# Two decoder layers on one core: the attention heads' projections and value rows as three rounded products instead of one f32 product, and where the splitting is done

## The reference, cut to what matters

```
a = h @ w_qkv_a
c_q  = rmsnorm(a[..., :384]);  c_kv = rmsnorm(a[..., 384:640]);  k_pe = rope(a[..., 640:])
q = (c_q @ w_q_b)              # per head: 128 plain columns, 64 rotary ones (then rope)
q_lat = q[..., :128] @ w_uk    # w_uk, w_uv: the two halves of a head's w_kv_b (256 x 256)
...
s = q_lat @ c_kv.T + q_pe @ k_pe.T;  p = softmax(causal(s * scale));  o = (p @ c_kv) @ w_uv
x = x + o @ w_o
```

## Time and profile before

| | us |
|---|---|
| median of 3 runs | 3307.57 |
| lowest, highest | 3305.08, 3314.09 |
| profiled execution, its own time | 3305.95 |
| span of the profiled execution | 3304.1 |
| TensorE busy | 3176.3 |
| VectorE, ScalarE, GpSimd busy | 1840.6, 1333.0, 1204.4 |

### The profile page before, as it was taken

The page is one execution under the profiler, slowest core; times in us unless marked ns, Lnnn a source line. Parts: engine busy times, 40 slices in busy tenths (PEclk is TensorE's granted clock), DMA queues, the critical chain, the costliest instruction groups (busy, mean ns, idle before and its releaser), DMA issues.

```text
span 3304.1 us, 69890 instructions
## 1 busy us (share of the span) xinstructions
PE 3176.3 (96%) x25744; PEld 2883.2 (87%) x25744; DVE 1840.6 (56%) x3139; ACT 1333.0 (40%) x2785; POOL 1204.4 (36%) x841
## 2 busy tenths in 40 slices
PE   8999999999999999999999999999999999999998
PEld 6688887687999999997999887877788899999998
DVE  3466663216544478757303377777734644457885
ACT  2244445512444533322213365566521354443332
POOL 0000000010766777731222222223213276677771
PEclk9999999999999999999999999999989999999999
DMA  3122224500444544432213201110152155454442
GB/s 112 43 79 66 69 74 147 179 13 20 151 157 157 184 133 142 133 109 69 90 53 114 99 14 34 33 40 27 31 170 51 46 164 157 157 184 141 140 141 77
DMA packets 306260, 330.39 MB, mean 100 GB/s; under 512 B 54350, under 2 KB 287745, under 8 KB 305954
## 3 DMA queue, kind: packets, MB, share of 16 engines
q1 hardware_dynamic: 300178, 308.64, 29.4%
q0 software_dynamic: 5904, 19.21, 1.8%
HBM read 232.05 MB, written 116.16 MB: 105 GB/s over the span
## 4 chain that ended last, share of the span: by engine, by line
PE 71%; DVE 8%; issue 6%; POOL 5%; PEld 3%; ACT 3%; SPq 2%; DMA 1%; DVEq 0%; POOLq 0%; PEldq 0%; ACTq 0%
PE bank L650 67%; PE bank L658 4%; PEld bank L650 3%; POOL wloA L2066 2%; POOL arena L2066 2%; DVE arena L3579 1%; SPq L1753 1%; DVE hT L3650 1%; POOL wloS L2066 1%; POOL table L2066 1%; SPq L1694 0%; SPq L1748 0%; DVE arena L3039 0%; DVE fb L3284 0%; DVE arena L3596 0%
## 5 line engine op out<-in xcount | busy, mean ns | idle before, releaser
L650 PE MATMUL bank<-arena 128*32 128x128 f32 (+18 forms) x7390 | 949.5, 317 | 37.5 <-DVE hT L3650 12.9
L650 PEld LDWEIGHTS bank<-arena 128*128 128x128 f32 (+9 forms) x7390 | 737.1, 166 | 223.0 <-issue 37.5
L2283 ACT COPY arena<-bank 128x512 f32<-128x512 f32 (+14 forms) x527 | 235.0, 484 | 627.8 <-PE bank L650 427.9
L2066 POOL TENSOR_TENSOR arena<-arena 128x512 f32<-128x512 f32 x120 | 164.9, 1374 | 605.0 <-PE bank L650 376.6
L2506 ACT ACTIVATE whiS<-arena 128x512 fp32r<-128x512 f32 x180 | 112.9, 627 | 406.8 <-POOL arena L2066 391.1
L2066 POOL TENSOR_TENSOR wloA<-arena,whiA 128x512 fp32r<-128x512 f32 x180 | 261.6, 1469 | 13.2 <-ACT whiA L2503 13.2
L2066 POOL TENSOR_TENSOR wloS<-arena,whiS 128x512 fp32r<-128x512 f32 x180 | 239.6, 1345 | 49.1 <-ACT whiS L2506 49.1
L3445 DVE TENSOR_TENSOR hT<-hT,bank 128x536 f32<-128x536 f32 x280 | 197.4, 706 | 80.6 <-PE bank L650 80.1
L658 PE MATMUL bank<-table,arena 128*128 128x128 f32 (+5 forms) x1422 | 181.4, 269 | 29.6 <-DVE arena L3159 13.1
L650 PE MATMUL bank<-hiT,whiS 128*128 128x268 f32 x768 | 199.2, 288 | 6.5 <-DVE loT L3284 3.7
L3289 DVE TENSOR_TENSOR arena<-std,bank 128x268 f32<-128x268 f32 x192 | 80.3, 431 | 219.2 <-PE bank L650 207.6
(11 more groups left out here) (320 smaller groups left out, 8533.1 us busy)
## 6 DMA issues: line engine op xcount, KB each, us to landing
u_scratch<-arena SPq DMA_DIRECT2D x480, 134.0 KB, 1.9
arena<-in_ffn_w_up SPq DMA_DIRECT2D x64, 512.0 KB, 4.1
arena<-u_scratch SPq DMA_DIRECT2D x56, 536.0 KB, 5.1
arena<-in_ffn_w_down SPq DMA_DIRECT2D x112, 256.0 KB, 4.2
arena<-u_scratch SPq DMA_DIRECT2D x56, 402.0 KB, 5.8
arena<-past_scratch SPq DMA_DIRECT2D x32, 640.0 KB, 7.0
past_scratch<-in_cache_kv_latent SPq DMA_DIRECT2D x128, 128.0 KB, 2.4
past_scratch<-in_cache_k_rope SPq DMA_DIRECT2D x128, 32.0 KB, 2.2
```

Source lines behind the costliest of these rows:

```text
L650: return pe.matmul(out, lhsT, rhs, start=first, stop=last, skip_group_check=group)
L2066: return pool.tensor_tensor(out, a, b, op)
L2283: lane.do(act.copy(dst, b if view is None else view(b)), ring.drained)
```

## The change

The latents `cq` and `ckv` and the head weights `wqp`, `wq`, `wkv` are split. The rounded parts lie where `hT` lay, the rests in place of the values. For this `hT` is stored to a DRAM scratch after the tokens have been turned in (SP, one DMA), ScalarE waits for that store before it rounds, and `hT` is loaded back in four quarters, one before `w_o` and three behind it; VectorE waits for each at the first add of a quarter.

ScalarE rounds `wqp` and the pieces of `cq` ahead of its copies of latent rows; VectorE takes their rests ahead of the meeting. After the meeting ScalarE rounds `wkv`, `ckv`, `wq`, and VectorE takes the rests between the raw queries' cosine product and the rotation. In the loop, in the second head of a pair, ScalarE rounds `wqp`, `wq`, `wkv` of the next pair at n = 7, 8, 9 ahead of the exponent, where it waits for the loads at n = 7, and VectorE takes the rests at n = 7, 8, 9 after `scaled(n - 1)`. The half of `wkv` that is turned for the sample queries stays whole; its rest has a tile of its own (`wkn_lo`). TensorE waits for the rests (`lo_s`) at `raw_queries` and, once, ahead of the first projections. GpSimd's wait counts the roundings that are new. The sample part keeps a copy of 64 columns of `ckv` (`ckv_new`). Left out below: places in the arena, tallies of the loops, and that copy's use.

```
@@ -55,7 +55,7 @@
 ROWS_AT = (0, 2, 3)
-DVE_HEADS = 44
+DVE_HEADS = 47
@@ -97,6 +97,7 @@
 
+LATENTS_AT = {"cq": 17152, "ckv": 20368, "wqp": 25424, "wq": 28080, "wkv": 29232}
@@ -270,6 +271,16 @@
         q2 = [exact(f"q2_{hh}", hh * T, T) for hh in range(2)]
+        cq_lo, ckv_lo = exact("cq_lo", LATENTS_AT["cq"], 3, T), exact("ckv_lo", LATENTS_AT["ckv"], 2, T)
+        wqp_lo, wq_lo, wkv_lo = [exact(f"{name}_lo", LATENTS_AT[name], *dims)
+                                 for name, *dims in (("wqp", 3, P), ("wq", 3, 384), ("wkv", 2, 512))]
+        cq_hi, ckv_hi = x_hi[:, 0:3, :], x_hi[:, 3:5, :]
+        xf, at = x_hi[:, :, :].rearrange("p k t -> p (k t)"), 5 * T
+        wq_hi, at = xf[:, at:at + 3 * 384].rearrange("p (k n) -> p k n", k=3), at + 3 * 384
+        wqp_hi, at = xf[:, at:at + 3 * P].rearrange("p (k n) -> p k n", k=3), at + 3 * P
+        wkv_hi, at = xf[:, at:at + 2 * 512].rearrange("p (k n) -> p k n", k=2), at + 2 * 512
+        wkn_lo, at = xf[:, at:at + 4 * NOPE].rearrange("p (k h n) -> p k h n", k=2, h=2), at + 4 * NOPE
+        assert at <= KT * T
...
@@ -553,7 +570,8 @@
         out_s, eps_s = sem("stored"), sem("eps_ready")
-        wq_s, wq_used, wkv_used = sem("w_q_loaded"), sem("w_q_used"), sem("w_kv_used")
+        wq_s, lo_s, wkv_used = sem("w_q_loaded"), sem("latents_and_weights_split"), sem("w_kv_used")
+        early_put, hidden_back = sem("normed_hidden_stored"), [(tile_s[0], 32), (tile_s[1], 16), (tile_s[2], 16), (tile_s[3], 48)]
...
@@ -781,11 +799,21 @@
 
-            def raw_queries():
-                wq_t.expect(64)
-                pe.wait_ge(wq_s, wq_t.value())
+            def projection(w_hi, w_lo, x_hi, x_lo, n, w):
+                b = rv.bank()
+                for k in range(n):
+                    mm(b[:, 0:w], w_hi(k), x_hi(k), k == 0, False)
+                    mm(b[:, 0:w], w_hi(k), x_lo(k), False, False)
+                for k in range(n):
+                    ins = mm(b[:, 0:w], w_lo(k), x_hi(k), False, k == n - 1)
+                rv.done(ins)
+
+            def raw_queries(n):
+                lo_t.expect(n)
+                pe.wait_ge(lo_s, lo_t.value())
                 for at, w in PIECES:
-                    product(rv, lambda j: wqp[:, j, :], lambda j: cq[:, j, at:at + w], 3, w=w)
+                    projection(lambda j: wqp_hi[:, j, :], lambda j: wqp_lo[:, j, :],
+                               lambda j: cq_hi[:, j, at:at + w], lambda j: cq_lo[:, j, at:at + w], 3, w)
@@ -796,8 +824,10 @@
                 at, w = PIECES[p]
-                product(rv, lambda j: wq[:, j, hh * 192:hh * 192 + NOPE], lambda j: cq[:, j, at:at + w], 3, w=w)
-                product(rv, lambda j: wkv[:, j, hh * 256:hh * 256 + NOPE], lambda j: ckv[:, j, at:at + w], 2, w=w)
+                projection(lambda j: wq_hi[:, j, hh * 192:hh * 192 + NOPE], lambda j: wq_lo[:, j, hh * 192:hh * 192 + NOPE],
+                           lambda j: cq_hi[:, j, at:at + w], lambda j: cq_lo[:, j, at:at + w], 3, w)
+                projection(lambda j: wkv_hi[:, j, hh * 256:hh * 256 + NOPE], lambda j: wkn_lo[:, j, hh, :],
+                           lambda j: ckv_hi[:, j, at:at + w], lambda j: ckv_lo[:, j, at:at + w], 2, w)
@@ -811,9 +841,13 @@
                         for t in range(n):
+                            out, rows = b[0:QT, t * VH:(t + 1) * VH], slice((t0 + t) * QT, (t0 + t + 1) * QT)
+                            v = slice(hh * 256 + NOPE, (hh + 1) * 256)
                             for k in range(2):
-                                ins = mm(b[0:QT, t * VH:(t + 1) * VH], ckv[:, k, (t0 + t) * QT:(t0 + t + 1) * QT],
-                                         wkv[:, k, hh * 256 + NOPE:(hh + 1) * 256], k == 0, k == 1)
+                                mm(out, ckv_hi[:, k, rows], wkv_hi[:, k, v], k == 0, False)
+                                mm(out, ckv_hi[:, k, rows], wkv_lo[:, k, v], False, False)
+                            for k in range(2):
+                                ins = mm(out, ckv_lo[:, k, rows], wkv_hi[:, k, v], False, k == 1)
@@ -871,7 +905,7 @@
                             if n == NQ:
-                                raw_queries()
+                                raw_queries(3)
@@ -888,8 +922,10 @@
 
-            raw_queries()
+            raw_queries(4)
             rotated(0)
+            lo_t.expect(5)
+            pe.wait_ge(lo_s, lo_t.value())
...
@@ -1724,6 +1760,9 @@
 
+            sp.wait_ge(a_drained, 10)
+            sp.wait_ge(v_drained, 10)
+            sp.dma_start(h_d[:, :], hx[:, :]).then_inc(early_put, 16)
@@ -1786,10 +1825,21 @@
 
+            def load_hidden(q):
+                s, l = QUARTERS[q]
+                at = l * TH + s * TS
+                sp.dma_start(hT[:, :, at:at + TS],
+                             h_d.rearrange("p (k t) -> p k t", k=KT)[:, :, at:at + TS]).then_inc(hidden_back[q][0], 16)
+
+            sp.wait_ge(early_put, 16)
+            load_hidden(0)
+
                 load(wo[half], w[:, 3 * half:3 + 5 * half, :], wo_t)
+            for q in (1, 2, 3):
+                load_hidden(q)
@@ -2055,7 +2105,7 @@
             for pair in range(H // 2):
-                pool.wait_ge(round_s, 14 * pair + 2)
+                pool.wait_ge(round_s, 17 * pair + 11)
@@ -2351,11 +2401,26 @@
             norm_t.expect(9)
+            def rounded(dst, src):
+                act.activation(dst, src, ACT.Copy).then_inc(round_s, 1)
+
+            wq_t = Tally(wq_s)
+            wq_t.expect(64)
+            act.wait_ge(early_put, 16)
+            act.wait_ge(wq_s, wq_t.value())
+            rounded(wqp_hi, wqp)
+            for p, (at, w) in enumerate(PIECES):
+                act.wait_ge(norm_s, 7 + p)
+                rounded(cq_hi[:, :, at:at + w], cq[:, :, at:at + w])
             exp_t, qpe_t = Tally(exp_s), Tally(turned_s)
+            rounded(wkv_hi, wkv)
+            for at, w in PIECES:
+                rounded(ckv_hi[:, :, at:at + w], ckv[:, :, at:at + w])
+            rounded(wq_hi, wq)
@@ -2397,6 +2462,14 @@
                             turn(n - 2)
+                        if hh == 1 and not last and n == 7:
+                            wq_t.expect(64)
+                            act.wait_ge(wq_s, wq_t.value())
+                            rounded(wqp_hi, wqp)
+                        if hh == 1 and not last and n == 8:
+                            rounded(wq_hi, wq)
+                        if hh == 1 and not last and n == 9:
+                            rounded(wkv_hi, wkv)
...
@@ -3094,8 +3169,24 @@
             norm(ckv, ckv, 2, R_KVN, mark["norm_kv"])
+            lane.settle()
+            lane.do(dve.tensor_copy(ckv_new, ckv[:, :, NP:T]))
+            round_t, lo_t = Tally(round_s), Tally(lo_s)
+
+            def rest(out, raw, hi):
+                return lane.do(dve.tensor_tensor(out, raw, hi.bitcast(F32), ALU.subtract), lo_t)
+
+            def rounded():
+                round_t.expect()
+                dve.wait_ge(round_s, round_t.value())
+
                 norm_piece(cq, cq, 3, R_QN, Tally(a_drained, mark["norm_q"][p]), *PIECES[p])
+            rounded()
+            rest(wqp_lo[:, :, :], wqp, wqp_hi)
+            for at, w in PIECES:
+                rounded()
+                rest(cq_lo[:, :, at:at + w], cq[:, :, at:at + w], cq_hi[:, :, at:at + w])
@@ -3112,7 +3203,14 @@
 
-            round_t = Tally(round_s)
+            def split_w_kv():
+                rounded()
+                value = [t.rearrange("p k (h a n) -> p k h a n", h=2, a=2)[:, :, :, 1, :] for t in (wkv_lo[:, :, :], wkv, wkv_hi)]
+                nope = [t.rearrange("p k (h a n) -> p k h a n", h=2, a=2)[:, :, :, 0, :] for t in (wkv, wkv_hi)]
+                for k in range(2):
+                    lane.do(dve.tensor_tensor(value[0][:, k], value[1][:, k], value[2][:, k].bitcast(F32), ALU.subtract))
+                    ins = dve.tensor_tensor(wkn_lo[:, k], nope[0][:, k], nope[1][:, k].bitcast(F32), ALU.subtract)
+                    lane.do(ins, lo_t if k == 1 else None)
@@ -3163,6 +3261,14 @@
                             scaled(n - 1)
+                        if hh == 1 and not last and n == 7:
+                            rounded()
+                            rest(wqp_lo[:, :, :], wqp, wqp_hi)
+                        if hh == 1 and not last and n == 8:
+                            rounded()
+                            rest(wq_lo[:, :, :], wq, wq_hi)
+                        if hh == 1 and not last and n == 9:
+                            split_w_kv()
@@ -3184,6 +3290,12 @@
             take_raw_queries()
+            split_w_kv()
+            for at, w in PIECES:
+                rounded()
+                rest(ckv_lo[:, :, at:at + w], ckv[:, :, at:at + w], ckv_hi[:, :, at:at + w])
+            rounded()
+            rest(wq_lo[:, :, :], wq, wq_hi)
...
@@ -3252,6 +3366,8 @@
                     s, l = QUARTERS[q]
+                    if layer == 0 and ks[0] == 0:
+                        dve.wait_ge(hidden_back[q][0], hidden_back[q][1] + 16)
```

(19 more changed lines are left out.)

## The result

The change has a median of 3332.84 us (3327.69 to 3333.3, five runs) against 3307.57 us: ratio 1.0074, 95% interval 1.0057 to 1.009. It is slower by 25 us. The profiled execution took 3327.69 us (span 3325.9, mean granted clock 0.986), against 3305.95 (3304.1, 0.991).

A forecast was written before the change was run, and what follows sets the result against it. TensorE was taken as the bound, with 71% of the chain. Ahead of the loop 11.2 us, pair 1 (13.6 - 11.2), pairs 2 and 3 2 x 2.3, pair 4 -0.45, clock 6: 23.7 on 3305.95 gives 3330 us, range 3318 to 3338.

The forecast's parts named there:

- Projections 0.613 to 0.49 us a step, value rows 0.22 to 0.27: TensorE products: three rounded ones save 0.125 us per projection or raw-query step, lose 0.05 us per value-row step.
- rival B: Value rows and projections: short rounded products follow their columns, 0.057 us for 128; with hidden splits 3292 us; chance 0.16.
- A first head shorter by 1.15, the last second head longer by 0.7: Head loop: a head's projections save 1.85 us, its value rows put 0.7 us on the path.
- Ahead of the loop 11.2: Before the head loop: meeting 6.9 us later, rests behind it 5.4 us less 1.1 from raw queries; 11.2 us in all.
- Raw queries 5.7 later, waiting 5 us, and 2 us of clock a time: Ends of pairs: raw queries wait for all three splits, 5.7 us later; half clock loses 2 us each, 6 in all.
- rival A: Head loop: the splits hide, so no 5.7 us delay and no clock term; 3308 us; chance 0.22.
- Pair 1: Next weights land at 247.0 behind the page gather; raw queries at 256.7, pair 2 begins 13.6 us late.
- At nothing: Hidden state's store, its way back and the up-weights: covered by other work, so no cost; without that cover 11 us.
- Rival D: Output projection: quarters of the hidden state or up-weights come late, +11 us, 3341 us; chance 0.02.
- C, a clock low for longer: Clock stays low through rotation, projection and first projections: 5 us a time, +9 to +13, 3341 us; chance 0.10.
- The sum: Whole kernel: delays ahead of and in the loop plus clock make 23.7 us more, 3330 us.

The follow-up runs named there:

- f32 run: Changed kernel with projections and raw queries as one f32 product of the rounded parts, rests left out of them, all splits kept: 3350.84 us, ratio 1.0134.
- the second store: Changed kernel with the store of the hidden state issued twice and waited for like the first: 3334.14 us, ratio 1.0088.
- the version with three repairs: Changed kernel with raw queries waiting only for their own split, latent copies ahead of roundings, 27 pages gathered before the first load: 3311.77 us, ratio 1.0015.

## Why the prediction was right, point by point

The prediction was 3330 us; 3332.84 was measured, inside the forecast's own range. The mechanism is the one foretold, and the terms are off by up to 1.5 us each. By its steps:

**Projections 0.613 to 0.49 us a step, value rows 0.22 to 0.27.** Value rows right. A projection step saves less than the 0.125 us foretold. At the high level rounded products start 0.175 us apart at 384 columns and 0.14 at 304, so three take 0.525 and 0.42 us, mean over the three pieces 0.49 as foretold. The f32 records start 0.32 us apart at 384 columns (before, 437.08, 437.40) and 0.26 at 304 (f32 run, 218.16, 218.42), two a step, so a step is 0.60 on the mean, not 0.613. That leaves 0.11 us, and the f32 run has 0.115 by its median, 0.10 in a pair of heads. The value-row products of after start 0.09 apart:
```profile
175.41 0.26 PE L668 MATMUL bank<-wkv_lo,x_hi 128*104 128x128 f32 x1
175.50 0.35 PE L668 MATMUL bank<-x_hi,ckv_lo 128*104 128x128 f32 x2
175.68 0.25 PE L668 MATMUL bank<-x_hi 128*104 128x128 f32 x1
```
With it rival B falls. The rule of the Trainium skill (TensorE: Matmul & The Clock Gate, "Wait — 56ns, not 53.3ns?"), start to start as the columns over 2.4 GHz plus 2.5 ns, would have given 0.056 us for 128 columns. That rule says nothing of weight loads, and here each product has one of its own; for such products the measured 0.09 us decides.

**A first head shorter by 1.15, the last second head longer by 0.7.** Measured 0.4, 0.8, 0.8 and 1.0 less, head by head, and 0.7 more (39.63 against 38.91). The first heads win less than foretold because a step saves less.

**Ahead of the loop 11.2.** Measured 12.7, with the 1.2 us of the earlier start. The meeting is 7.9 us behind the norm, not 6.9: I had counted ScalarE's copies at their old pace, but behind transposes at half clock they are slower. That term, 1 us, was missing. Behind the meeting 4.8 us are added instead of 4.3: VectorE's rests are seen as the 4.42 us wait, and the other half microsecond was not taken apart (the first raw queries ran at half clock there).

**Raw queries 5.7 later, waiting 5 us, and 2 us of clock a time.** Measured 4.7, 5.2 and 5.2 us of waiting; in pair 3 the raw queries start 6.1 us later within their head than before, of which the head's value rows have 0.7. The clock costs 2 us by the run with TensorE kept busy, and 3.85 us of work lay at the low level for the 4 foretold. Pairs 2 and 3 grew by 4.7 and 4.4, foretold 2.3 + 2. This says that rival A (the splits hide) was wrong: they did not, though they do in the run that waits for the own split.

**Pair 1.** Foretold 2.4 + 2, measured 3.9; raw queries at 255.7, foretold 256.7. The load held ScalarE 1.75 us at n = 7 (until 246.75, foretold 247.0), less than the 3.1 of the sum, and TensorE's wait behind it was 4.7 us.

**At nothing:** the store, the way back and the up-weights. Right; no wait of TensorE or VectorE for the hidden state is seen up to 900 us, and the second store changed nothing. Rival D falls.

**C, a clock low for longer:** it wasn't. A stretch of 21 us around the raw queries has a mean of 0.84, which would be 6.7 us at half, but the part of it that holds work is 3.85 us in pair 3 (462.15 to 466.00); the other part lies in the wait, where the clock has fallen already and costs nothing. At half speed 3.85 us lose 1.9.

**The sum.** 23.7 foretold. The heads were 25.5 late with the start counted, and the medians differ by 25.3. The profiled executions differ by 21.7 only, because 4 us came back later at places that the change doesn't touch.

What I had priced too high is the gain once the waits are gone: a pair then won 1.1 us, not the 3.4 of rival A. By the f32 run the 39 steps of a pair give 3.8 us; less 1.4 for the value rows and 0.7 for the wait for the copied queries, 1.7; the last 0.6 us stay open. In the forecast sum this hardly shows, since the gain is small beside the waits; its larger error is the 1.5 us ahead of the loop. With f32 value rows a pair wins 2.9 us.

## What to carry to other kernels

Three rounded products beat one f32 product when they are long (here at 304 and 384 columns) and lose when they are short (at 128, where the start to start is the same as at 104); change each shape by its own price. A split is an extra station between loading and use: let each consumer wait for its own part only, keep the roundings behind copies that release another engine, and give the rests to an engine that is idle. A wait of 5 us on TensorE cost two more here, for the clock behind it.

## What the runs showed of the hardware that was not expected

Rounded products with weights of their own start 0.09 us apart at 104 and 128 columns, 0.12 at 256 and 268, 0.14 at 304, 0.175 at 384: the first two are no different. The 6.12 us in which the transposes were held left TensorE at half clock, and there ScalarE's copies fell into its pace, 0.87 us a copy instead of 0.53 (5.83 us for 11), so that a low clock on TensorE lengthened a meeting that TensorE doesn't bound otherwise. And GpSimd's rest of 1152 columns took 2.63 us, beside VectorE's 1.36, at no cost to the heads (head 0 takes 46.01 us with it, 45.87 in the version with three repairs).
